# Half-array pairs for the gated layers' up slabs and Strassen products, with the products between an up slab's two passes

## The chip, the cores and the metric

The kernel runs on one core of a Trainium2 chip. The metric is the device time of one execution in microseconds, here the median of three runs. The engines are TensorE (PE; the profile shows its weight loads apart as PEld), VectorE (DVE), ScalarE (ACT), GpSimd (POOL) and SyncE (SP, which issues the DMAs). All of them work through their own instruction streams in order and meet only at semaphores.

## The reference, cut to what matters

A decoder trunk of two layers on 512 tokens of width 1024, in fp32. Each layer is a gated feed-forward half, a mixer, and another gated half; after each the residual sum is normalised:

```
def swiglu(x, w1, w3, w2):
    return (jax.nn.silu(x @ w1) * (x @ w3)) @ w2

h = swiglu(x, ffn_w1[l, 0], ffn_w3[l, 0], ffn_w2[l, 0])      # w1, w3: 1024 x 2816, w2: 2816 x 1024
x = layer_norm(DEEPNORM_ALPHA * x + FFN_RES_WEIGHT * h, ln_g[l, 0], ln_b[l, 0])
```

The mixer of layer 0 is windowed and block-sparse attention, that of layer 1 a gated linear recurrence. The change touches only the four gated (swiglu) layers.

## The kernel before, in words

**Numbers.** Every fp32 operand of the large products is split into a high part of type fp32r (ACT copies it) and a low part, the difference (POOL or DVE subtracts). A product is then three matmuls into one PSUM bank: high by high, high by low, low by high (`three`, L1480 to L1484). All have 128 rows, 128 stationary columns and 512 moving columns in the stretches that matter here. PE loads the stationary operand anew for each.

**A gated layer.** The 2816 hidden features are cut into 11 groups of 256 (`NG`). For each group there is an up slab of w1 (1024 x 256) and one of w3: `up` (L1510) multiplies its two halves j = 0, 1 of 128 features, 8 chunks of the contraction by three matmuls each, 24 matmuls into bank b0 + j, 48 for the slab. w1 slabs use banks 0 and 1, w3 slabs banks 2 and 3. ACT turns banks 0 and 1 into the gate (`gates`, L769), DVE multiplies banks 2 and 3 with it into the hidden tiles (`hiddens`, L1004), into `hid` and `hid_odd` by turns.

The down products of the first eight groups go by Strassen's scheme in Winograd's form. Two groups make one p (p = 0 to 3). The left operand is split into A11, A12, A21, A22 (hidden features by token halves), the right one, two down slabs, into B11 to B22; DVE makes the sums S1 to S4 and T1 to T4 (`left_sum` L1019, `right_sum` L1035), ACT the high parts (L779, L788), DVE the low parts (`left_low` L1025, `right_low` L1041). Seven products P1 to P7 replace eight: each (`product`, L1517) is 12 matmuls, 6 for each of two token tiles t, tile t into bank b0 + t, the banks being 4, 5 and 6, 7 by turns. DVE then adds them to x or keeps them (`add_product` L1057, `keep_product` L1066 and L1069). At p = 3 `combine_kept` follows.

**Order on PE** (L1821 on), with s0 the layer's first slab: slabs 0 to 3, then for each p: slab 4p+4, P1, P2; slab 4p+5, P6, P5; slab 4p+6, P7, P3; slab 4p+7, P4. Then come the last slabs and the ordinary down products. Before each piece PE waits for the operands' counts (`lo_ready` for a slab; `left_lo_ready` and `right_lo_ready` for a product) and for its banks (`gate_done`, `hid_done`, `product_added`).

**Order on the others.** DVE, from the end of slab 4p+3: two hidden tiles, sums S1, S3, S2, low part of A12, sum S4, add P4 of the p before, low parts of S1, B11, S2, S3, S4, A22, the four right sums, then keep P1, add P2, low parts T2, T1; after slab 4p+5: two hidden tiles, low part of the next A11 (at p = 3 of a whole hidden tile instead), keep P6, low T3, add P5, low B22, add P7 and P3, low T4 and the next B21. ACT: high parts in the same order, the gates, and the high copy of one slab (L755) in four places of each p; the copy of slab s waits until the slab two before has released its slot (`w_free`). POOL: the low part of each slab in four quarters (L684, `low`), in order, as soon as ACT has made the high part. SP loads slabs as their buffers come free.

Of the kernel before, what the change touches and what calls it, by code (L numbers as in the profile page):

```python
# [31 lines left out]
P = 128  # L32
# [4 lines left out]
DC = D // P  # L37
GW = 256
NG = DFF // GW
# [10 lines left out]
HALF_CHUNK = 64  # L50
# [11 lines left out]
NP = 4  # L62
# [5 lines left out]
PRODUCTS = ["P1", "P2", "P6", "P5", "P7", "P3", "P4"]  # L68
LEFT = {"P1": "A11", "P2": "A12", "P3": "S4", "P4": "A22", "P5": "S1", "P6": "S2", "P7": "S3"}
# [132 lines left out]
def build_trunk(nc, x_in, w1, w3, w2, ln_g, ln_b, aw_in, sinks, aw_out, hw_in, hnorm, hw_out, lbs_in, out,  # L202
# [7 lines left out]
    for n, ph in enumerate(phases):  # L210
        s0 = bases[n][0]
# [14 lines left out]
    with ExitStack() as ctx:  # L226
# [3 lines left out]
        def sem(name):  # L230
            return ctx.enter_context(nc.semaphore(name))
# [132 lines left out]
        right_lo_ready = sem("right_lo_ready")  # L364
        product_done = sem("product_done")
        product_added = sem("product_added")
        kept_combined = sem("kept_combined")
        y_added = sem("y_added")
        par_loaded = [sem(f"par_loaded{i}") for i in range(2)]
# [50 lines left out]
        def added_count(f, p, name, i):  # L420

            return N_ADDED * (NP * f + p) + ADDED[name] + i

        def left_count(f, p, name):

            return 7 * (NP * f + p) + LEFT_ORDER.index(name) + 1

        def right_count(f, p, name):

            return 7 * (NP * f + p) + RIGHT_ORDER.index(name) + 1  # L430
# [1048 lines left out]
        def _(pe):  # L1479
            def three(out_, w, xs, first, last):  # L1480

                pe.matmul(out_, w[0], xs[0], start=first, stop=False)  # L1482
                pe.matmul(out_, w[0], xs[1], start=False, stop=False)  # L1483
                return pe.matmul(out_, w[1], xs[0], start=False, stop=last)  # L1484
# [29 lines left out]
                    pe.wait_ge(freed, 2 * G - 1 + j)  # L1514
                    features(bank[b0 + j], slot_of[s], j, slice(0, T)).then_inc(done, 1)

            def product(n, f, p, name, b0):  # L1517

                a_hi_, a_lo_ = left_parts(LEFT[name])
                b_hi_, b_lo_ = right_parts(n, RIGHT[name])  # L1520
                pe.wait_ge(left_lo_ready, left_count(f, p, LEFT[name]))
                pe.wait_ge(right_lo_ready, right_count(f, p, RIGHT[name]))
                at = PRODUCTS.index(name)
                q, last_user = (p, PRODUCTS[at - 2]) if at >= 2 else (p - 1, ("P4", "P3")[at])
                for t in range(2):
                    tok = slice(t * P, (t + 1) * P)
                    if q >= 0:
                        n_targets = (2, 1)[last_user not in ("P5", "P7")]
                        pe.wait_ge(product_added, added_count(f, q, last_user, n_targets * (t + 1)))
                    for c in range(2):  # L1530
                        mm = three(bank[b0 + t][:], (a_hi_[:, c, tok], a_lo_[:, c, tok]),
                                   (b_hi_[:, c, :], b_lo_[:, c, :]), c == 0, c == 1)
                    mm.then_inc(product_done, 1)

            def keep_clock(times):

# [276 lines left out]
            for n, (kind, _, _, _) in enumerate(phases):  # L1813
                s0, K0, H0 = bases[n]
                if kind == "ffn":
# [4 lines left out]
                    up(s0 + 3, G0 + 1, up3_done, hid_done, 2)  # L1820
                    for p in range(NP):  # L1821
                        G = G0 + 2 * p + 2
                        up(s0 + 4 * p + 4, G, up1_done, gate_done, 0)
                        product(n, fi, p, "P1", 4)
                        product(n, fi, p, "P2", 6)
                        up(s0 + 4 * p + 5, G, up3_done, hid_done, 2)
                        product(n, fi, p, "P6", 4)
                        product(n, fi, p, "P5", 6)
                        up(s0 + 4 * p + 6, G + 1, up1_done, gate_done, 0)
                        product(n, fi, p, "P7", 4)  # L1830
                        product(n, fi, p, "P3", 6)
                        up(s0 + 4 * p + 7, G + 1, up3_done, hid_done, 2)
                        product(n, fi, p, "P4", 4)

                    G = G0 + NG - 1
                    up(s0 + UPS - 1, G, up1_done, gate_done, 0)
# [77 lines left out]
```

## Time and profile before

| | us |
|---|---|
| median of 3 runs (lowest to highest) | 1984.76 (1984.67 to 1986.42) |
| the profiled execution, whole | 1986.88 |
| its span in the trace | 1984.8 |
| PE busy | 1951.8 (98%) |
| weight loads busy (beside matmuls) | 1657.4 (84%) |
| DVE busy | 1090.4 (55%) |
| ACT busy | 631.9 (32%) |
| POOL busy | 909.4 (46%) |

Busy times are unions over an engine's instructions, so overlapping matmuls are not counted twice. A matmul's duration in the profile runs from its start until its result is in PSUM; since matmuls are pipelined, what one costs is read from the distance between two starts. The granted clock is given as a share of full speed: 1.00 is 2.4 GHz, 0.50 is 1.2 GHz.

### The profile page before, as it was taken

The numbers are of one execution on the slowest core, as the hardware profiler recorded it, in microseconds if no ns is written. First come the engines' busy times: TensorE is split into PE (matmuls) and PEld (weight loads), VectorE is DVE, ScalarE is ACT, GpSimd is POOL, SyncE is SP. The second block draws the span as 40 slices with busy tenths as digits, with TensorE's granted clock in tenths as the row PEclk, the third lists the DMA queues.
The fourth block names the chain that finished last, engine by engine and source line by source line (L and its number), as shares of the span: only waits on it lengthen the run. The fifth ranks groups of instructions, "written<-read, shape, count | busy, mean of one in ns | idle before, by whom it ended". The sixth has DMA issues, their size and how long they took to land.

```text
span 1984.8 us, 26090 instructions
## 1 busy us (share of the span) xinstructions
PE 1951.8 (98%) x10825; PEld 1657.4 (84%) x10825; DVE 1090.4 (55%) x1492; ACT 631.9 (32%) x789; POOL 909.4 (46%) x600
## 2 busy tenths in 40 slices
PE   8999999999999999999999999999999999999997
PEld 8888888978878888888988888898988888888886
DVE  2756472544364766563575647265544774656545
ACT  3333232253422333322333323232232223323321
POOL 4454464632314455355445446453433344365534
PEclk9999999999999999999999999999999999999999
DMA  6232323221104232232423132332221204333221
GB/s 236 97 107 71 128 85 106 90 69 60 64 22 149 85 106 94 98 106 85 149 85 106 64 128 85 106 100 71 68 83 65 64 28 143 107 98 114 92 79 43
DMA packets 135589, 185.52 MB, mean 93 GB/s; under 512 B 3232, under 2 KB 119088, under 8 KB 135472
## 3 DMA queue, kind: packets, MB, share of 16 engines
q1 hardware_dynamic: 135312, 183.59, 27.9%
q8 instruction: 86, 1.41, 0.3%
q10 hardware_dynamic: 160, 0.26, 0.1%
q14 instruction: 31, 0.25, 0.0%
HBM read 181.48 MB, written 2.10 MB: 92 GB/s over the span
## 4 chain that ended last, share of the span: by engine, by line
PE 94%; DVE 4%; DMA 1%; ACT 0%; issue 0%; SPq 0%; POOL 0%; DVEq 0%; ACTq 0%
PE psum L1482 30%; PE psum L1483 29%; PE psum L1484 29%; PE psum L1771 2%; PE psum L1743 1%; PE psum L1710 1%; PE psum L1506 1%; PE psum L1725 1%; DVE x L1097 1%; DMA raw<-in_ffn_w 1%; DVE arena L1199 0%; DVE arena L1200 0%; PE psum L1799 0%; DVE x L1276 0%; PE psum L1809 0%
## 5 line engine op out<-in xcount | busy, mean ns | idle before, releaser
L684 POOL TENSOR_TENSOR w_lo<-raw,w_hi 128x512 fp32r<-128x512 f32 x524 | 849.1, 1652 | 921.6 <-ACT w_hi L755 897.1
L1482 PE MATMUL psum<-xt_hi,w_hi 128*128 128x512 f32 (+1 forms) x1824 | 676.3, 371 | 2.6 <-DVE xt_lo L996 1.2
L1484 PE MATMUL psum<-xt_hi,w_lo 128*128 128x512 f32 (+1 forms) x1824 | 671.5, 368 | 0.0
L1483 PE MATMUL psum<-xt_lo,w_hi 128*128 128x512 f32 (+1 forms) x1824 | 671.5, 368 | 0.0
L1482 PEld LDWEIGHTS psum<-xt_hi,w_hi 128*128 128x128 f32 x1824 | 344.4, 189 | 65.1 <-issue 4.0
L1484 PEld LDWEIGHTS psum<-xt_hi,w_lo 128*128 128x128 f32 x1824 | 344.3, 189 | 57.4
L1483 PEld LDWEIGHTS psum<-xt_lo,w_hi 128*128 128x128 f32 x1824 | 344.5, 189 | 55.8
L755 ACT ACTIVATE w_hi<-raw 128x2048 fp32r<-128x2048 f32 x132 | 251.8, 1911 | 325.8 <-PE psum L1484 323.9
L1057 DVE SCALAR_TENSOR_TENSOR x<-psum,x 128x512 f32<-128x512 f32 x224 | 145.6, 684 | 131.5 <-PE psum L1484 128.3
L769 ACT ACTIVATE gate<-psum 128x512 f32<-128x512 f32 x88 | 52.5, 597 | 308.8 <-PE psum L1484 308.8
L1097 DVE SCALAR_TENSOR_TENSOR x<-psum,x 128x512 f32<-128x512 f32 x128 | 85.9, 687 | 108.5 <-PE psum L1484 108.2
L1482 PE MATMUL psum<-w_hi,h_hi 128*128 128x512 f32 x352 | 140.1, 398 | 2.9 <-DVE x L1097 2.8
L1482 PE MATMUL psum<-w_hi,xt_hi 128*128 128x256 f32 (+2 forms) x448 | 140.7, 314 | 0.0
L1483 PE MATMUL psum<-w_lo,h_hi 128*128 128x512 f32 x352 | 138.4, 393 | 0.0
L1484 PE MATMUL psum<-w_hi,xt_lo 128*128 128x256 f32 (+2 forms) x448 | 137.4, 307 | 0.0
L1483 PE MATMUL psum<-w_lo,xt_hi 128*128 128x256 f32 (+2 forms) x448 | 137.3, 306 | 0.0
L1484 PE MATMUL psum<-w_hi,h_lo 128*128 128x512 f32 x352 | 137.1, 390 | 0.0
L1483 PE MATMUL psum<-w_lo,a_hi 128*128 128x512 f32 x320 | 126.1, 394 | 0.0
L1482 PE MATMUL psum<-w_hi,a_hi 128*128 128x512 f32 x320 | 125.4, 392 | 0.0
L1484 PE MATMUL psum<-w_hi,a_lo 128*128 128x512 f32 x320 | 124.2, 388 | 0.0
L1041 DVE TENSOR_TENSOR w_lo<-raw_odd,w_hi 128x1024 fp32r<-128x1024 f32 x48 | 59.1, 1231 | 110.5 <-ACT w_hi L788 110.5
L1004 DVE TENSOR_TENSOR hid<-psum,gate 128x512 f32<-128x512 f32 x48 | 33.2, 691 | 151.2 <-PE psum L1484 151.2
(168 smaller groups left out, 2199.1 us busy)
## 6 DMA issues: line engine op xcount, KB each, us to landing
raw<-in_ffn_w SPq DMA_DIRECT2D x115, 1024.0 KB, 5.4
raw_odd<-in_ffn_w SPq DMA_DIRECT2D x16, 1024.0 KB, 5.1
raw<-in_hgrn_w_in SPq DMA_DIRECT2D x16, 1024.0 KB, 5.4
raw<-in_attn_w_in SPq DMA_DIRECT2D x9, 1024.0 KB, 5.3
raw<-in_attn_w_out SPq DMA_DIRECT2D x4, 1024.0 KB, 4.9
raw<-in_hgrn_w_out SPq DMA_DIRECT2D x4, 1024.0 KB, 4.9
lng<-in_ln_g SPq DMA_DIRECT2D x6, 512.0 KB, 4.2
lnb<-in_ln_b SPq DMA_DIRECT2D x6, 512.0 KB, 5.9
```

The source lines that it names most:

```text
L684: op = pool.tensor_tensor(w_lo[:, slot_of[s], cols], raw[:, slot_of[s], cols], w_hi[:, slot_of[s], cols].bitcast(F32), ALU.subtract)
L755: act.activation(w_hi[:, slot_of[s], :], raw[:, slot_of[s], :], ACT.Copy).then_inc(hi_ready, 1)
L769: act.activation(gate[:, j, :], bank[j][:], ACT.Silu).then_inc(gate_done, 1)
L1004: dve.tensor_tensor(dst[:, j, :], bank[2 + j][:], gate[:, j, :], ALU.mult).then_inc(hid_done, 1)
L1041: dve.tensor_tensor(lo, right_source(n, name), hi.bitcast(F32), ALU.subtract).then_inc(right_lo_ready, 1)
L1057: dve.scalar_tensor_tensor(out=x_piece(row, t, half), in0=bank[b0 + t][:], scalar=weight / ALPHA, in1=x_piece(row, t, half), op0=ALU.mult, ...
L1097: dve.scalar_tensor_tensor(out=part, in0=banks[k % len(banks)][:], scalar=weight / ALPHA, in1=part, op0=ALU.mult, op1=ALU.add).then_inc(y_ ...
L1482: pe.matmul(out_, w[0], xs[0], start=first, stop=False)
L1483: pe.matmul(out_, w[0], xs[1], start=False, stop=False)
L1484: return pe.matmul(out_, w[1], xs[0], start=False, stop=last)
L1506: mm = pe.transpose(bank[4 + 2 * (t % 2) + b][:, c * P:(c + 1) * P], x[:, t, (4 * b + c) * P:(4 * b + c + 1) * P], ident[:])
L1771: mm = pe.matmul(out_, ks[:, g % 2, h, keys], rhs, start=True, stop=True)
```

## The change

`three` is kept for everything else. For slabs 4p+4 to 4p+7 and for all seven products each full matmul becomes two matmuls over 64 of the 128 rows. A new helper, `crossed`, emits them in pairs: one of the pair uses rows 0 to 63 and one output bank, the other rows 64 to 127 and the other output bank. In the first pass output o = 0 takes the lower rows and o = 1 the upper, in the second pass the other way round, so that after both passes each bank holds the sum over all 128 rows. The second pass waits for a semaphore that the last matmul of the first raises. Both banks' `done` counts are raised together at the end of the second pass. Between the two passes of a slab stand the first passes of its products, and after the slab's second pass the products' second passes. Operands and free banks are waited for before the first pass, for both outputs at once.

```diff
--- before.py
+++ after.py
@@ -364,6 +364,9 @@
         right_lo_ready = sem("right_lo_ready")
         product_done = sem("product_done")
         product_added = sem("product_added")
+        up1_half_done = sem("up1_half_done")
+        up3_half_done = sem("up3_half_done")
+        product_half_done = sem("product_half_done")
         kept_combined = sem("kept_combined")
         y_added = sem("y_added")
         par_loaded = [sem(f"par_loaded{i}") for i in range(2)]
@@ -1514,23 +1517,57 @@
                     pe.wait_ge(freed, 2 * G - 1 + j)
                     features(bank[b0 + j], slot_of[s], j, slice(0, T)).then_inc(done, 1)
 
-            def product(n, f, p, name, b0):
+            def crossed(outs, operands, steps, second):
+
+
+                for c in range(steps):
+                    for a, b in ((0, 0), (0, 1), (1, 0)):
+                        for o in range(2):
+                            half = 1 - o if second else o
+                            rows = slice(half * HALF_CHUNK, (half + 1) * HALF_CHUNK)
+                            w, xs = operands(o, c)
+                            mm = pe.matmul(outs[o][:], w[a][rows], xs[b][rows],
+                                           start=not second and c == 0 and a + b == 0,
+                                           stop=second and c == steps - 1 and a == 1)
+                return mm
+
+            def up_half(second, s, f, G, done, half_done, freed, b0):
+
+                if second:
+                    pe.wait_ge(half_done, 2 * NP * f + G - NG * f - 1)
+                else:
+                    pe.wait_ge(lo_ready, s + 1)
+                    pe.wait_ge(freed, 2 * G)
+                slot = slot_of[s]
+
+                def operands(j, c):
+                    cols = slice(c * GW + j * P, c * GW + (j + 1) * P)
+                    return (w_hi[:, slot, cols], w_lo[:, slot, cols]), (xt_hi[:, c, :], xt_lo[:, c, :])
+
+                mm = crossed((bank[b0], bank[b0 + 1]), operands, DC, second)
+                mm.then_inc(*((done, 2) if second else (half_done, 1)))
+
+            def product_half(second, n, f, p, name, b0):
 
                 a_hi_, a_lo_ = left_parts(LEFT[name])
                 b_hi_, b_lo_ = right_parts(n, RIGHT[name])
-                pe.wait_ge(left_lo_ready, left_count(f, p, LEFT[name]))
-                pe.wait_ge(right_lo_ready, right_count(f, p, RIGHT[name]))
                 at = PRODUCTS.index(name)
-                q, last_user = (p, PRODUCTS[at - 2]) if at >= 2 else (p - 1, ("P4", "P3")[at])
-                for t in range(2):
-                    tok = slice(t * P, (t + 1) * P)
+                if second:
+                    pe.wait_ge(product_half_done, 7 * (NP * f + p) + at + 1)
+                else:
+                    pe.wait_ge(left_lo_ready, left_count(f, p, LEFT[name]))
+                    pe.wait_ge(right_lo_ready, right_count(f, p, RIGHT[name]))
+                    q, last_user = (p, PRODUCTS[at - 2]) if at >= 2 else (p - 1, ("P4", "P3")[at])
                     if q >= 0:
                         n_targets = (2, 1)[last_user not in ("P5", "P7")]
-                        pe.wait_ge(product_added, added_count(f, q, last_user, n_targets * (t + 1)))
-                    for c in range(2):
-                        mm = three(bank[b0 + t][:], (a_hi_[:, c, tok], a_lo_[:, c, tok]),
-                                   (b_hi_[:, c, :], b_lo_[:, c, :]), c == 0, c == 1)
-                    mm.then_inc(product_done, 1)
+                        pe.wait_ge(product_added, added_count(f, q, last_user, 2 * n_targets))
+
+                def operands(t, c):
+                    tok = slice(t * P, (t + 1) * P)
+                    return (a_hi_[:, c, tok], a_lo_[:, c, tok]), (b_hi_[:, c, :], b_lo_[:, c, :])
+
+                mm = crossed((bank[b0], bank[b0 + 1]), operands, 2, second)
+                mm.then_inc(*((product_done, 2) if second else (product_half_done, 1)))
 
             def keep_clock(times):
 
@@ -1820,17 +1857,21 @@
                     up(s0 + 3, G0 + 1, up3_done, hid_done, 2)
                     for p in range(NP):
                         G = G0 + 2 * p + 2
-                        up(s0 + 4 * p + 4, G, up1_done, gate_done, 0)
-                        product(n, fi, p, "P1", 4)
-                        product(n, fi, p, "P2", 6)
-                        up(s0 + 4 * p + 5, G, up3_done, hid_done, 2)
-                        product(n, fi, p, "P6", 4)
-                        product(n, fi, p, "P5", 6)
-                        up(s0 + 4 * p + 6, G + 1, up1_done, gate_done, 0)
-                        product(n, fi, p, "P7", 4)
-                        product(n, fi, p, "P3", 6)
-                        up(s0 + 4 * p + 7, G + 1, up3_done, hid_done, 2)
-                        product(n, fi, p, "P4", 4)
+                        for second in (False, True):
+                            up_half(second, s0 + 4 * p + 4, fi, G, up1_done, up1_half_done, gate_done, 0)
+                            product_half(second, n, fi, p, "P1", 4)
+                            product_half(second, n, fi, p, "P2", 6)
+                        for second in (False, True):
+                            up_half(second, s0 + 4 * p + 5, fi, G, up3_done, up3_half_done, hid_done, 2)
+                            product_half(second, n, fi, p, "P6", 4)
+                            product_half(second, n, fi, p, "P5", 6)
+                        for second in (False, True):
+                            up_half(second, s0 + 4 * p + 6, fi, G + 1, up1_done, up1_half_done, gate_done, 0)
+                            product_half(second, n, fi, p, "P7", 4)
+                            product_half(second, n, fi, p, "P3", 6)
+                        for second in (False, True):
+                            up_half(second, s0 + 4 * p + 7, fi, G + 1, up3_done, up3_half_done, hid_done, 2)
+                            product_half(second, n, fi, p, "P4", 4)
 
                     G = G0 + NG - 1
                     up(s0 + UPS - 1, G, up1_done, gate_done, 0)
```

## Rows read from the trace of the kernel before

**Rows 1.** Part 1 of the page: busy us, share, instructions.

```profile
PE 1951.8 (98%) x10825; PEld 1657.4 (84%) x10825; DVE 1090.4 (55%) x1492; ACT 631.9 (32%) x789; POOL 909.4 (46%) x600
```

**Rows 2.** Part 4 of the page: chain that ended last, by engine.

```profile
PE 94%; DVE 4%; DMA 1%; ACT 0%; issue 0%; SPq 0%; POOL 0%; DVEq 0%; ACTq 0%
```

**Rows 3.** Windows: window, length, busy by engine, clock, DMA share, GB/s.

```profile
59.61:321.48 261.87, 261.87 (x1153) 216.26 (x1152) 158.05 (x187) 85.65 (x90) 130.55 (x68) 1.00 0.29 96
```

**Rows 4.** Timeline of PE (start, length): slab 4 and P1, first matmuls.

```profile
59.62 0.39 PE L1482 MATMUL psum<-xt_hi,w_hi 128*128 128x512 f32 x1
...
70.50 0.39 PE L1482 MATMUL psum<-w_hi,h_hi 128*128 128x512 f32 x1
```

**Rows 5.** Timeline of PE: 256-column matmuls, first and last of 43.

```profile
380.78 0.28 PE L1484 MATMUL psum<-xt_hi,w_lo 128*128 128x256 f32 x1
...
385.81 0.28 PE L1484 MATMUL psum<-xt_hi,w_lo 128*128 128x256 f32 x1
```

**Rows 6.** Timeline of PE: P4 first, next slab first, 12 matmuls apart.

```profile
182.36 0.39 PE L1482 MATMUL psum<-w_hi,a_hi 128*128 128x512 f32 x1
...
185.11 0.39 PE L1482 MATMUL psum<-xt_hi,w_hi 128*128 128x512 f32 x1
```

**Rows 7.** Groups of PE by form: scores (count, busy us, mean ns).

```profile
L1710 PE MATMUL psum<-arena 64*128 64x512 f32 x16 | 4.5, 641 | 0.0
...
L1710 PE MATMUL psum<-arena 64*128 64x384 f32 x16 | 3.7, 535 | 0.0
```

**Rows 8.** Timeline of PE and PEld: scores on alternating halves, merged.

```profile
540.27 1.13 PE L1710 MATMUL psum<-arena 64*128 64x512 f32 x4
...
549.06 0.93 PE L1710 MATMUL psum<-arena 64*128 64x128 f32 x8
549.16 0.42 PEld L1710 LDWEIGHTS psum<-arena 64*128 64x128 f32 x6
```

**Rows 9.** Timeline of DVE and POOL, p = 0 of the first layer.

```profile
59.88 0.69 DVE L1004 TENSOR_TENSOR hid_odd<-psum,gate 128x512 f32<-128x512 f32 x1 [4.75 <-PE psum L1484]
...
62.43 1.79 DVE L1025 TENSOR_TENSOR h_lo<-hid_odd,h_hi 128x512 fp32r<-128x512 f32 x1
...
67.54 2.31 DVE L1041 TENSOR_TENSOR w_lo<-raw,w_hi 128x1024 fp32r<-128x1024 f32 x1
...
61.87 6.89 POOL L684 TENSOR_TENSOR w_lo<-raw,w_hi 128x512 fp32r<-128x512 f32 x4 [14.08 <-ACT w_hi L755]
```

**Rows 10.** Timeline of DVE, beginning of p = 2.

```profile
182.63 0.69 DVE L1004 TENSOR_TENSOR hid_odd<-psum,gate 128x512 f32<-128x512 f32 x1 [0.97 <-PE psum L1484]
...
188.18 1.22 DVE L1041 TENSOR_TENSOR w_lo<-raw,w_hi 128x1024 fp32r<-128x1024 f32 x1
...
195.34 2.10 DVE L1035 TENSOR_TENSOR raw_odd<-raw_odd,raw 128x1024 f32<-128x1024 f32 x1
```

**Rows 11.** Timeline of POOL: slab 4p+5 of p=2, two quarters.

```profile
188.26 8.11 POOL L684 TENSOR_TENSOR w_lo<-raw,w_hi 128x512 fp32r<-128x512 f32 x1 [13.56 <-ACT w_hi L755]
...
199.82 1.30 POOL L684 TENSOR_TENSOR w_lo<-raw,w_hi 128x512 fp32r<-128x512 f32 x1
```

**Rows 12.** Timeline of PE: first matmul of slab 4p+5, p = 2.

```profile
201.48 0.39 PE L1482 MATMUL psum<-xt_hi,w_hi 128*128 128x512 f32 x1
```

**Rows 13.** Timeline of DVE, p=2: hidden tile of slab 4p+5, B22.

```profile
212.63 0.69 DVE L1004 TENSOR_TENSOR hid<-psum,gate 128x512 f32<-128x512 f32 x1 [4.37 <-PE psum L1484]
...
221.11 1.21 DVE L1041 TENSOR_TENSOR w_lo<-raw_odd,w_hi 128x1024 fp32r<-128x1024 f32 x1
```

**Rows 14.** Timeline of DVE, p = 3: the same two.

```profile
275.38 0.69 DVE L1004 TENSOR_TENSOR hid<-psum,gate 128x512 f32<-128x512 f32 x1 [4.75 <-PE psum L1484]
...
285.57 1.21 DVE L1041 TENSOR_TENSOR w_lo<-raw_odd,w_hi 128x1024 fp32r<-128x1024 f32 x1
```

**Rows 15.** Timeline: PE after its longest idle; window there (columns: group 3).

```profile
1370.55 0.64 PE L1771 MATMUL psum<-arena 128*64 128x32 f32 x8 [2.66 <-DVE arena L1201]
...
1370.00:1376.80 6.80, 6.25 (x42) 5.26 (x43) 3.80 (x8) 0.00 (x0) 2.90 (x3) 0.50 0.36 117
```

## The prediction

> **What bounds the kernel now.** I read the busy line first [rows 1]: TensorE (PE) is busy 98% of the span, and PE makes up 94% of the chain that ended last [rows 2]. In the four gated layers the stretch that the change touches is full: from slab 4 of the first layer to its first down product PE is busy 261.87 of 261.87 us at clock 1.00 [rows 3], and the other three are alike. So two things can move the time: what a matmul costs, and whether PE still finds its operands when it asks for them.
>
> What one costs: 48 matmuls of 512 columns start between 59.62 and 70.50 us, 226.7 ns apart [rows 4]. 42 intervals of 256-column ones take 380.78 to 385.81 us, 119.8 each [rows 5]. So 256 more columns cost 106.7 ns. 512 columns stream in 213.3, which is the level of 2.4 GHz at one column per cycle, and 13.3 ns are left between two weights. A Strassen product of 12 matmuls runs from 182.36 to 185.11: 229 ns each [rows 6].
>
> **What a pair of half matmuls costs.** Changed are 64 up slabs (4 per p, 4 p, 4 layers) of 48 matmuls, 3072, and 112 products of 12, 1344. Each becomes two 64-row matmuls on different halves and banks. Columns per half are as many as before, so a pair never takes less than 213.3, and at best 13.3 (15.7 in a product) are saved: 3072 x 13.3 + 1344 x 15.7 = 62 us. The nearest rows are the attention scores, 64-row matmuls of plain fp32 on alternating halves and two banks, where each is two instructions. From 384 to 512 columns their mean grows by 106 ns [rows 7], so they stream half as fast (427 for 512). Four that stream 853 ns a half lie within 1.13 us, eight that stream 640 within 0.93 [rows 8]: the halves do run together. Both carry the same first load and last drain, the one has 1 change of weights, the other 3: 1.13 - 0.853 = 0.277, 0.93 - 0.640 = 0.290, so 13 ns for two changes, 6.5 each. Bounds: 213.3 (change fully hidden) and 226.7 (these are fp32, and the 13.3 may belong to the fp32r operands). I take 213.3 + 6.5 = 219.8, by these rows. Gain: 3072 x 6.9 + 1344 x 9.2 = 34 us, 8.4 a layer.
>
> The trace's 226.7 also stands against a rule. The Trainium skill ("TensorE: Matmul & The Clock Gate", Back-to-back issue gap) has 512/2.4 + 2.5 = 215.8 ns between matmuls at the high clock; no row here shows that for 512 columns, and were a pair to reach it, the gain would be 51 us.
>
> **What the new order asks of the other engines.** One p is four slots: slab 4p+4 with P1, P2; 4p+5 with P6, P5; 4p+6 with P7, P3; 4p+7 with P4. Before, a product started after its whole slab, 10.88 us into the slot. Its first half now starts after half the slab, 24 x 0.2198 = 5.28 us in, and needs all its operands then. A half product takes 1.32, a slot 15.83, the last 13.19 (before 16.37 and 13.63). The operands come from queues of ACT, DVE and POOL that nothing shortens. I lay them against PE.
>
> *p = 0, P1.* The chain begins at slab 3, which is untouched: DVE starts the second hidden tile at 59.88, and right_low of B11 starts at 67.54 and takes 2.31, to 69.85 [rows 9]. Before, P1 asked at 70.50, 0.65 later. Now it asks at 59.62 + 5.28 = 64.9, and waits 5.0 us. Behind it in PE's queue stand P2, the slab's second pass and everything else, and no buffer or other work fills the hole. DVE is late because it shares its port: POOL works on slab 5 from 61.87, and DVE's operations of 0.68 take 1.79 [rows 9].
>
> *Boundary, p = 1 to 3.* Count from the end U of the second pass of the last slab (4p+7 of the p before). P4's second half ends at 1.32, the next slab's first pass at 6.60: there P1 asks. Slot 2 asks for slab 4p+5 at 1.32 + 15.83 = 17.15. Before, the hidden tile j=0 was done long before, and j=1 began 0.27 after the slab (182.36 to 182.63 [rows 6, 10]). Now both are released together, so j=1 begins at 0.27 + 0.60 = 0.87. From it DVE runs without a pause: B11's low part starts 5.55 after j=1 and takes 1.22 (188.18), so it is ready at 7.64 and P1 waits 1.1. Then come four left and four right sums, the last ending at 197.44, 14.8 after j=1 [rows 10]. Under these POOL's first quarter of slab 4p+5, released by ACT's high copy, took 8.11 us where the last took 1.30, and the slab was ready at 201.12, 18.5 after j=1 [rows 11]. PE used it at 201.48 [rows 12]: a slack of 0.36. Now 0.87 + 18.5 = 19.4 against 17.15: 2.25 us late. The wait of P1 lies within that, so it counts once. ACT is some 0.6 earlier, since P4 ends earlier after the slab, so POOL may come just as DVE reads PSUM and get the port at once. Then B11 becomes late as at p = 0 (two operations longer by 1.1 each: P1 waits 3.3) and the slab is in time. Ends 1.1 and 3.3; I take 2.25.
>
> *Slot 3, P3.* Before, B22's low part starts 8.48 after the hidden tile and takes 1.21, so it ends 9.69 after [rows 13]. That tile's chain is started by ACT's high copy, which the slab's end releases, so it isn't shifted by the 0.60. In the new slot 2 the slab ends at 13.19, B22 is ready at 13.19 + 0.27 + 9.69 = 23.15, and P3 asks at 15.83 + 5.28 + 1.32 = 22.43: 0.8 late with the wait's own latency. At p = 3 the two low parts of a whole hidden tile stand ahead (10.19 + 1.21 = 11.4 after, [rows 14]): 1.7 more, 2.5.
>
> Nothing else is late: P6 asks for T2 2 us or more after it is ready, P4 for T4 1.4 after; B21 comes 7.3 after T4, before the hidden tiles. The gates, now two at a time, are a slot ahead. Slabs 4p+6 to 4p+8 had 7 us or more to spare. A slab's weights come free 2.3 us later, which only 4p+5 could feel, and its copy waits for other work anyway. SP's loads hang on low parts that move with PE. The second pass's wait on the first (half_done) is covered by the products between them, 1.3 us or more; without that it would cost the drain, 0.39 - 0.21 = 0.18 us each.
>
> Stalls a layer: 5.0 + 3 x 2.25 + 3 x 0.8 + 2.5 = 16.7; four layers 67 us, twice the gain.
>
> *Clock.* After the one idle stretch of PE of 2.66 us (it ended at 1370.55) the granted clock is 0.50, 1.2 GHz, from 1370.0 to 1376.8 [rows 15]. The 5.0 us hole of p = 0 is longer. At half clock 3.4 to 6.8 us of work cost 1.7 to 3.4 more; bounds 0 and 3.4, I take 2.5: 10 us for four. Changes between full and half arrays, eight of them: about 0.1 each by the load no longer hidden, 1 us.
>
> **Sum.** -34 + 67 + 10 + 1 = +44 us. The profiled execution took 1986.88 (span 1984.8), 2 above the median 1984.76 of the three timed. 1986.88 + 44 = 2031; against the median 2029. I forecast 2028.
>
> **Rivals.**
> *Change of weights wholly hidden (213.3).* Gain 62. The halves' loads may overlap the other half's stream entirely. But PE then asks earlier: P1 5.1 late, the boundary 16.64 against 19.4 (2.75), slot 3 1.05, at p = 3 2.75: 19.3 a layer, 77. -62 + 77 + 11 = +26: 2011.
> *No cheaper pair (226.7).* Gain 3, from the products only; stalls 4.75 + 3 x 1.7 + 3 x 0.5 + 2.2 = 13.6 a layer, 54. +62: 2047. For it: 13.3 was only seen with fp32r, 6.5 only with fp32. It would also come about if half loads ran one after the other, about 0.11 each, twice in a pair. Against: six score loads of 0.19 lie in 0.42 us [rows 8], 0.115 a pair. The Trainium skill (same page, LDWEIGHTS) says that a load costs by its columns, not its rows, so that the change doubles the loading; by those rows the two loads of a pair overlap.
> *The port falls the other way (not slower).* If at p = 0 POOL is starved as it is at 188.26, DVE's operations stay at 0.6 to 1.2 and P1 waits 1.8; if at the boundary POOL gets in during DVE's PSUM reads and gives way again, slab 4p+5 is in time and 1.1 is left. Stalls 1.8 + 3.3 + 2.4 + 2.5 = 10 a layer, holes too short for the clock: at 219.8 that is 40 - 34 + 1 = +7. With 213.3, 46 - 62 + 1 = -15: 1970. It decides from a pair price of about 217.7 down. Against: at p = 0 the order on ACT, DVE and POOL is untouched.
> *The halves take turns.* Each half matmul at 226.7: 4416 x 226.7 = +1000 us, 2985. Only possible if fp32r behaves unlike the scores, which write each PSUM column at half the rate.
>
> **How the numbers follow.** Forecast 56%, its own range 2012 to 2048 (stalls 1.1 to 3.3 at twelve boundaries, clock 0 to 14). Fully hidden 14%, no cheaper 10%, port 15%, turns 5%. Range 1998 to 2060, which holds the first three with their spread (longer holes at boundaries may drop the clock too). 0.2% is about what a measurement can tell. Faster: 11 of the port's 15. Same: 3 of them. Slower: the rest, 86%.
>
> **What would show it.** In the changed profile: (1) a pair's starts 219.8 apart, its two matmuls some 7 ns apart; (2) an idle of 5.0 us of PE before P1 of p = 0, ended by DVE w_lo L1041, in each layer; (3) idle before slot 2 of p = 1 to 3, ended by POOL's low part, and a shorter one before P1; (4) 0.8 and 2.5 us before P3, ended by DVE; (5) a clock of 0.50 after the hole (2). PE without idle in the stretch, whatever the pair costs, would prove me wrong; so would pairs above 227.

## The result and the profile after

The changed kernel takes 2067.85 us (three runs, 2065.39 to 2069.22) against 1984.76 before: ratio 1.0415, 95% interval 1.0395 to 1.0436. It is slower by 83 us; the forecast was 2028, slower by 43, with a range up to 2060. The direction was right, and most of the places where PE waits; the size was not.

The page's busy line, after (compare [rows 1]), and its chain by engine ([rows 2]):

```profile
PE 1980.5 (96%) x15241; PEld 1786.6 (86%) x15241; DVE 1121.4 (54%) x1492; ACT 619.2 (30%) x789; POOL 838.8 (41%) x600
...
PE 89%; DVE 7%; issue 3%; ACT 1%; DMA 0%; SPq 0%; POOL 0%; DVEq 0%; ACTq 0%
```

PE has 4416 matmuls more and is busy 28.7 us more, in a span that is 81 us longer: most of the loss is idle. Windows of the first gated layer (length, then busy time of PE, PEld, DVE, ACT, POOL, clock, DMA share, GB/s), the first from its slab 4 to its first down product ([rows 3] before):

```profile
59.47:343.01 283.54, 270.63 (x2257) 247.36 (x2257) 165.87 (x187) 82.40 (x90) 113.15 (x68) 0.98 0.28 89
68.59:75.41 6.82, 5.71 (x27) 4.86 (x29) 6.78 (x8) 0.00 (x0) 0.00 (x0) 0.50 0.52 154
269.97:273.38 3.41, 3.41 (x20) 3.08 (x18) 3.41 (x3) 0.00 (x0) 3.37 (x3) 0.50 0.00 0
307.52:310.93 3.41, 3.41 (x19) 3.18 (x16) 3.38 (x6) 0.00 (x0) 0.00 (x0) 0.50 0.51 174
```

The stretch grew from 261.87 to 283.54 us: 13 us without a matmul, and three windows at half clock. Over four layers the same stretches are longer by 21.7, 19.8, 21.7 and 19.1, 82 us together, which is the whole difference.

What a pair costs, PE's timeline (each row is the two halves of a pair, their starts 10 ns apart):

```profile
84.09 0.40 PE L1529 MATMUL psum<-xt_hi,w_hi 64*128 64x512 f32 x2
84.31 0.40 PE L1529 MATMUL psum<-xt_lo,w_hi 64*128 64x512 f32 x2
...
84.99 0.40 PE L1529 MATMUL psum<-xt_lo,w_hi 64*128 64x512 f32 x2
```

The halves do run together, but a pair starts every 226.7 ns, the distance of the full matmuls before ([rows 4]): a half-slab of 24 pairs takes 5.44 us, a product 2.75. Nothing is gained.

The holes, that is, the stretches in which PE stands idle (PE, then DVE): P1 at p = 0, P1 at p = 1, and P3 at p = 3.

```profile
64.84 0.39 PE L1529 MATMUL psum<-xt_hi,w_lo 64*128 64x512 f32 x2
69.70 0.79 PE L1529 MATMUL psum<-w_hi,h_hi 64*128 64x512 f32 x2 [4.48 <-DVE w_lo L1044]
...
135.59 0.43 PE L1529 MATMUL psum<-xt_hi,w_lo 64*128 64x512 f32 x2
137.87 0.50 PE L1529 MATMUL psum<-w_hi,h_hi 64*128 64x512 f32 x2 [1.84 <-issue]
...
306.99 0.50 PE L1529 MATMUL psum<-w_hi,a_hi 64*128 64x512 f32 x2 [1.87 <-DVE w_lo L1044]
```

```profile
67.28 2.28 DVE L1044 TENSOR_TENSOR w_lo<-raw,w_hi 128x1024 fp32r<-128x1024 f32 x1
...
134.86 0.68 DVE L1028 TENSOR_TENSOR a_lo<-left_sum,a_hi 128x512 fp32r<-128x512 f32 x1
135.46 2.31 DVE L1044 TENSOR_TENSOR w_lo<-raw,w_hi 128x1024 fp32r<-128x1024 f32 x1
```

At p = 0 DVE ends B11's low part at 69.56 and P1 starts at 69.70 (forecast: 5.0 late; a start-to-start distance of 4.86, less the 0.23 of a pair, is 4.6). At the boundary between two p the low part ends at 137.77, P1 starts at 137.87, though the profile names no releaser ("issue"). POOL came in just before it:

```profile
134.90 7.42 POOL L687 TENSOR_TENSOR w_lo<-raw,w_hi 128x512 fp32r<-128x512 f32 x4 [11.64 <-ACT w_hi L758]
```

Against [rows 11], where the first quarter alone took 8.11, all four take 7.42. This time POOL is not held up, so slab 4p+5 is ready over 6 us early, and B11's low part is longer by 1.1. That is the case which the prediction gave as its upper end of 3.3, but one operation is longer, not two, and the wait is 2.0. POOL began while DVE was ending an addition that reads PSUM (at 134.94); that this is what let it in is argued, no run tests it.

### The profile page after: what moved, and what is told of

The parts are those of the page before. It is cut to its first block, busy times and chain, and to the rows that moved or that the text cites. A ratio compares the mean times of both kernels' runs of the same rounds, so it can differ in the third digit from the quotient of the medians.

```text
span 2065.8 us, 34922 instructions
## 1 busy us (share of the span) xinstructions
PE 1980.5 (96%) x15241; PEld 1786.6 (86%) x15241; DVE 1121.4 (54%) x1492; ACT 619.2 (30%) x789; POOL 838.8 (41%) x600
## 4 chain that ended last, share of the span: by engine, by line
PE 89%; DVE 7%; issue 3%; ACT 1%; DMA 0%; SPq 0%; POOL 0%; DVEq 0%; ACTq 0%
PE psum L1529 47%; PE psum L1485 12%; PE psum L1486 12%; PE psum L1487 12%; PE psum L1808 2%; PE psum L1780 1%; PE psum L1747 1%; DVE w_lo L1044 1%; PE psum L1509 1%; PE psum L1762 1%; DVE x L1100 1%; DMA raw<-in_ffn_w 0%; DVE arena L1202 0%; DVE arena L1203 0%; DVE x L1060 0%
## 5 line engine op out<-in xcount | busy, mean ns | idle before, releaser
L1529 PE MATMUL psum<-xt_hi,w_hi 64*128 64x512 f32 x2048 | 432.8, 388 | 0.0
L1529 PE MATMUL psum<-xt_lo,w_hi 64*128 64x512 f32 x2048 | 431.3, 387 | 0.0
L1529 PE MATMUL psum<-xt_hi,w_lo 64*128 64x512 f32 x2048 | 431.2, 387 | 0.0
L1485 PE MATMUL psum<-xt_hi,w_hi 128*128 128x512 f32 (+1 forms) x800 | 278.0, 348 | 2.9 <-DVE w_lo L1353 1.2
L1487 PE MATMUL psum<-xt_hi,w_lo 128*128 128x512 f32 (+1 forms) x800 | 272.8, 341 | 0.0
L1486 PE MATMUL psum<-xt_lo,w_hi 128*128 128x512 f32 (+1 forms) x800 | 272.7, 341 | 0.0
L1529 PEld LDWEIGHTS psum<-xt_hi,w_hi 64*128 64x128 f32 x2048 | 225.3, 185 | 14.6 <-issue 1.4
L1529 PEld LDWEIGHTS psum<-xt_lo,w_hi 64*128 64x128 f32 x2048 | 225.0, 185 | 13.0
L1529 PEld LDWEIGHTS psum<-xt_hi,w_lo 64*128 64x128 f32 x2048 | 224.2, 184 | 13.0
L1485 PEld LDWEIGHTS psum<-xt_hi,w_hi 128*128 128x128 f32 x800 | 151.8, 190 | 26.6 <-issue 5.4
```

The lines of the kernel that those rows point to most:

```text
L1529: mm = pe.matmul(outs[o][:], w[a][rows], xs[b][rows], start=not second and c == 0 and a + b == 0, stop=second and c == steps - 1 and a == 1)
```

## The experiments

**Order or halves?** The first pair of kernels separates the change's two parts. e1 keeps the new order and has full matmuls:

```diff
-                for c in range(steps):
+                for c in range(steps // 2 * second, steps // 2 * (second + 1)):
                     for a, b in ((0, 0), (0, 1), (1, 0)):
                         for o in range(2):
-                            half = 1 - o if second else o
-                            rows = slice(half * HALF_CHUNK, (half + 1) * HALF_CHUNK)
...
-                            mm = pe.matmul(outs[o][:], w[a][rows], xs[b][rows],
+                            mm = pe.matmul(outs[o][:], w[a], xs[b],
```

> The changed kernel's order kept exactly (slab in two passes, the first passes of its products between them, operands and banks waited for before the first pass, both banks' counts raised at the end), but with full 128-row matmuls: a pass takes half of the contraction's chunks for both outputs. Theory (a pair of halves costs just what a full matmul costs, and all of the loss is the order): no difference from the changed kernel, 2068 us (2060 to 2076), with the same idle before P1 at p = 0 (about 4.7 us) and at the boundaries (about 2.0 us). Rival (the halves themselves cost something, in loads, drains or clock): clearly below 2060, by what they cost.

2065.43 us (ratio to before 1.0409, 1.0392 to 1.0426), and the hole before P1 stands at 4.73 us idle. PE's timeline at the hole:

```profile
68.94 0.70 PE L1526 MATMUL psum<-w_hi,h_hi 128*128 128x512 f32 x2 [4.73 <-DVE w_lo L1044]
```

The halves can be taken away and the loss stays: it is the order's. e2 keeps the halves and has the old order:

```diff
                         for second in (False, True):
                             up_half(second, s0 + 4 * p + 4, fi, G, up1_done, up1_half_done, gate_done, 0)
+                        for second in (False, True):
                             product_half(second, n, fi, p, "P1", 4)
                             product_half(second, n, fi, p, "P2", 6)
```

(and so for the other three slabs).

> Half-array pairs as in the changed kernel, but each slab's second pass follows its first at once, and the products come after the whole slab as before the change. Theory (order is the cause): before 1984.8, minus 3 for the products at 226.7, plus 5 waits of a second pass on the first per p that nothing covers now (4 slabs and P4), 80 in all at about 0.2 us: 16, plus some 4 at the boundaries where both hidden tiles are still released together and at mode changes: 2001 us (1994 to 2010), without the 4.7 us hole. Rival (half pairs are the cause): stays near 2068.

2016.28 (ratio 1.0157, 1.0142 to 1.0173), 31 us above before, where I had expected 16. The holes are gone and no window in the layers is at half clock. PE's timeline where a slab's second pass begins:

```profile
64.42 0.39 PE L1529 MATMUL psum<-xt_hi,w_lo 64*128 64x512 f32 x2
64.87 0.50 PE L1529 MATMUL psum<-xt_hi,w_hi 64*128 64x512 f32 x2
65.20 0.40 PE L1529 MATMUL psum<-xt_lo,w_hi 64*128 64x512 f32 x2
```

The rest is this uncovered wait: the two steps take 0.45 and 0.33 us instead of 0.23 each, and a slab's 48 pairs take 11.24 us for 10.88. So a second pass that nothing covers costs 0.36 us and not 0.2; 80 of them are 29 us. The drain (the end of a matmul's recorded duration, in which the next one could already stream), by which I had sized it, is only half of what it costs: the weight loads, which elsewhere start with the matmul before, start here only after the wait.

**What the holes do to the clock.** e4 puts half-array matmuls of no use in front of P1's and P3's waits, where PE was idle:

```diff
                 else:
+                    fill = {("P1", 0): 19, ("P3", 3): 7}.get((name, p), 7 if name == "P1" else 0)
...
+                    for i in range(fill):
+                        for o in range(2):
+                            rows = slice(o * HALF_CHUNK, (o + 1) * HALF_CHUNK)
+                            pe.matmul(bank[6 + o][:], xt_hi[rows, i % 8, 0:P], xt_hi[rows, i % 8, :],
+                                      start=True, stop=True)
                     pe.wait_ge(left_lo_ready, left_count(f, p, LEFT[name]))
```

> The changed kernel with half-array matmuls of no use put before P1 (19 pairs at p = 0, 7 else) and before P3 at p = 3 (7), where PE stood idle; into banks 6 and 7, which are free. They end before the operands come. Theory (the holes drop the clock, and the time at 1.2 GHz after them costs 20 us: half of 39 us of work in the ten windows at 0.50 within the changed stretches): 2048 us (2042 to 2055), no window at 0.50 in those stretches. Rival (the clock's drops come from elsewhere or cost little): within 4 us of 2068.

2051.14 (ratio 1.0332, 1.0316 to 1.0347): 16.7 less than the changed kernel, by doing more. The first layer's window has clock 1.00 throughout:

```profile
59.10:340.00 280.90, 278.00 (x2362) 248.72 (x2362) 166.20 (x188) 84.77 (x93) 113.30 (x68) 1.00 0.28 91
```

So the half clock after the holes cost some 17 to 20 us, where the prediction had 10: 17 is the whole gain of e4, and its waits are some 3 us longer than the changed kernel's. Each layer's stretch is still 16.4 longer than before: 65 us for the waits themselves.

**Why DVE is late at p = 0.** e7 moves one ACT copy, and with it POOL's work on slab 5:

```diff
-                        if p == 0:
-                            high(s0 + 5)
                         left_high(fi, p, "A12")
...
                         for name in ("S2", "S3", "S4", "A22"):
                             left_high(fi, p, name)
+                        if p == 0:
+                            high(s0 + 5)
```

> The changed kernel with one move: at p = 0 ACT copies slab 5 (and so releases POOL's part of it) after the high parts of S2 to A22 and not before A12's. Theory (the hole at p = 0 is so long because POOL's subtraction shares DVE's port while DVE makes B11's operands): DVE's operations up to B11 take 0.6 and 1.2 us, B11 is ready about 3 us earlier, the hole before P1 shrinks from 4.7 to about 1.6 us and stops dropping the clock (some 2.4 us more a layer): 2068 - 4 x 5.4 = 2046 us (2042 to 2058). Rival (DVE is slowed by something else, such as ACT's copies or PE's reads): the hole stays 4 us or more, 2064 to 2070.

2045.72 (ratio 1.0307, 1.0291 to 1.0322). DVE's timeline, from the hidden tile on:

```profile
58.69 0.69 DVE L1007 TENSOR_TENSOR hid_odd<-psum,gate 128x512 f32<-128x512 f32 x1 [4.75 <-PE psum L1487]
...
61.22 0.69 DVE L1028 TENSOR_TENSOR h_lo<-hid_odd,h_hi 128x512 fp32r<-128x512 f32 x1
61.83 0.68 DVE L1022 TENSOR_TENSOR hid_odd<-hid_odd,hid 128x512 f32<-128x512 f32 x1
62.43 0.69 DVE L1028 TENSOR_TENSOR a_lo<-left_sum,a_hi 128x512 fp32r<-128x512 f32 x1
63.03 1.22 DVE L1044 TENSOR_TENSOR w_lo<-raw,w_hi 128x1024 fp32r<-128x1024 f32 x1
```

B11 is ready 5.56 us after the hidden tile begins, where it took 9.9 to 10.0 with POOL at work beside it ([rows 9]). That it is POOL and not ACT shows in the same rows: ACT copies high parts in both kernels while DVE works, and DVE's operations are long only while POOL subtracts (61.63 to 68.47 in the changed kernel; here POOL begins at 65.68). So the time of an operand is set by another engine's work beside it. The 4.3 us gained are more than the 3 I had expected, and P1 is only 0.3 late. In exchange slab 5 itself is now late, 0.4 us of idle in each layer.

**Are the holes only the queues' order?** e5 leaves PE as changed and reorders ACT and DVE:

```diff
-                        left_low(fi, p, "A12")
-                        left_sum(fi, p, "S4")
                         if p:
                             add_product(fi, p - 1, "P4", 4, [(1, 0)], weight)
+                            right_low(n, fi, p, "B11")
+                        left_low(fi, p, "A12")
+                        left_sum(fi, p, "S4")
                         left_low(fi, p, "S1")
-                        right_low(n, fi, p, "B11")
```

(ACT alike; at p = 0 B11's low part stands before the loop; the low part of the next A11, at p = 3 of a whole hidden tile, moves behind B22's.)

> The changed kernel, PE's order untouched; only ACT and DVE are reordered: B11's high and low part before A12's (at p = 0 before the hidden tiles), the addition of P4 ahead of them, and the low part of the next A11 (at p = 3 of a whole hidden tile) behind B22's. Theory (the holes are these queues' order): the holes before P1 (4.7 us at p = 0, 2.0 else) and before P3 go, and with them the windows at half clock; as a pair costs what a full matmul costs, the time comes back to that of before and no further: 1984 to 1992 us, if slab 4p+5 stays in time; if POOL now starves as it did before the change, up to 2 us at each of 12 boundaries come back: up to 2016. Rival (the holes move to the next operand, P2's or T2): above 2030.

1996.78 (ratio 1.0067, 1.005 to 1.0083): 71 of the 83 us are back, and no window of the layers is at half clock. That is above the 1984 to 1992 expected. What is left is 12 waits of 0.5 us or a little more at p = 1 to 3, before P5's first half in slot 2, one of 1.0 and small ones. The profile names no releaser for them:

```profile
145.22 0.43 PE L1530 MATMUL psum<-w_hi,a_lo 64*128 64x512 f32 x2
146.00 0.51 PE L1530 MATMUL psum<-w_hi,a_hi 64*128 64x512 f32 x2 [0.34 <-issue]
```

It ends above the kernel before: when a pair costs what a full matmul costs, nothing can bring it below.

**Where the 13.3 ns lie.** They are the excess of a matmul's 226.7 ns over the 213.3 in which its columns stream. Two probes stand behind the last down product of the kernel before; each kind has 18 to 36 matmuls, pairs or quadruples.

```diff
                     last_downs(n, s0 + UPS + 2, K0 + 1, H0 + 2)
+                        for i in range(36):
+                            pe.matmul(bank[2], st(LO, i), mv(LO, i), start=True, stop=True)
+                            pe.matmul(bank[3], st(HI, i), mv(HI, i), start=True, stop=True)
...
```

> The kernel before, with extra matmuls of 512 columns behind its last down product, each kind 18 to 36 times from operands that lie in SBUF (its output is untouched). Distance between starts read for each. Theory (the 13.3 ns beside the 213.3 of streaming belong to every fp32r matmul in every row group that it uses): full array with the same stationary operand each time 227, alternating banks 227, pair of halves 227 a pair, one half alone 227, four 32-row groups 227 a quadruple, 64 stationary columns 227; plain fp32 full arrays and pairs both about 427 + 6 an instruction. Rival A (the 13.3 are the change of the stationary operand): less with the same operand or with 64 columns. Rival B (they are the bank's): less where banks alternate. The Trainium skill (TensorE: Matmul & The Clock Gate, Back-to-back issue gap) gives 215.8 for a moving operand of 512 columns; if the type makes the 13.3, the bf16 cases show it, full and paired.

PE's timeline, merged by line (banks by turns; one half alone; four 32-row groups; 64 stationary columns; contiguous bf16):

```profile
1987.71 8.32 PE L1852 MATMUL psum<-xt_hi,w_hi 128*128 128x512 f32 x36
...
2004.28 8.32 PE L1857 MATMUL psum<-xt_hi,w_hi 64*128 64x512 f32 x36
2012.53 5.76 PE L1861 MATMUL psum<-xt_hi,w_hi 32*128 32x512 f32 x96
2018.21 8.49 PE L1863 MATMUL psum<-xt_hi,w_hi 128*64 128x512 f32 x36
2026.78 7.72 PE L1865 MATMUL psum<-xt_hi,w_hi 128*128 128x512 bf16 x35
```

Less the last one's 0.39 and divided by the steps between, these are 226.6 with alternating banks, 226.6 for one half alone, and 215.9 for bf16 (its row has 35 of 36). Where the kind changes, the first step can be longer; from the second start on it is 227 for a quadruple of row groups and 230 with 64 columns. The same stationary operand each time gave 226.7, pairs of bf16 halves 216, plain fp32 429.1 an instruction full and 429.2 in halves. So it is neither the change of weights nor the bank nor the number of rows. The 215.8 of the Trainium skill (TensorE: Matmul & The Clock Gate, Back-to-back issue gap) holds here for contiguous bf16 and not for fp32r.

Is it the type? e8 and e9 below use bf16 at a stride of 4 bytes, where a matmul took 225. The second probe tells type and stride apart:

> A second probe behind the kernel before, full arrays, 24 to 36 matmuls of each kind. In e9 the cross terms, bf16 read at a stride of 4 bytes, took 225 ns each, and the first probe's contiguous bf16 216. Theory (the 10 ns or more beyond streaming go with how far the moving operand's 512 elements are spread, 2048 bytes a row, whatever the type): bf16 with a strided moving operand and contiguous stationary 225, with a contiguous moving and a strided stationary 216; fp32r with one column repeated 512 times (stride 0) near 216; fp32r at a stride of 8 bytes 227 or more. Rival (it is the type, and in e9 the stationary stride costs the 9 ns): the other way round for the two bf16 cases, and 227 for fp32r at every stride. 384 and 256 columns of fp32r: 160 + 13 = 173 and 120 as in the kernel if the excess is per matmul, 170 and 113 if it is per column.

```profile
1979.66 8.30 PE L1851 MATMUL psum<-xt_hi,w_hi 128*128 128x512 bf16 x36
1987.80 7.93 PE L1854 MATMUL psum<-xt_hi,w_hi 128*128 128x512 bf16 x36
1995.38 16.59 PE L1857 MATMUL psum<-xt_hi,w_hi 128*128 128x512 f32 x36
...
2008.63 2.89 PE L1857 MATMUL psum<-xt_hi,w_hi 128*128 128x512 f32 x6
...
2011.79 8.03 PE L1859 MATMUL psum<-xt_hi,w_hi 128*128 128x512 f32 x36
2019.66 6.43 PE L1861 MATMUL psum<-xt_hi,w_hi 128*128 128x384 f32 x36
2025.92 4.47 PE L1863 MATMUL psum<-xt_hi,w_hi 128*128 128x256 f32 x36
2030.23 4.26 PE L1865 MATMUL psum<-xt_hi,w_hi 128*128 128x256 bf16 x36
```

In this order: bf16 with a strided moving operand 226, bf16 with a strided stationary operand 216, fp32r at a stride of 8 bytes 452 (the six from its middle; its first step takes 0.60), fp32r with one column repeated 218, fp32r with 384 columns 174, with 256 120, bf16 strided with 256 columns 113. So at 512 columns the excess of fp32r and of bf16 goes with how the moving operand lies in memory, 4 bytes from element to element, and not with which of the two types it is; at 8 bytes a matmul takes twice as long. In fp32r the excess is the same for 512, 384 and 256 columns (13 to 14 ns), but in strided bf16 it is 12 to 13 at 512 and 7 at 256: what sets it with fewer columns stays open. Plain fp32 lies 4 bytes apart as well and has an excess of only 2.5 over its 426.7; there each column takes two cycles. Both halves of the array read moving operands that are spread in the same way. That this is why a pair keeps the 13.3 fits the pairs of contiguous bf16, which come to 216; strided pairs of bf16 were not run.

**A faster version.** If the type were the cause, the cross terms could be read as bf16 from the words that are there. These kernels ran before the second probe. e6 does it in each triple, on the kernel before. A bf16 keeps the upper 16 bits of the word:

```diff
+                def top(part):
+                    return part.bitcast(mybir.dt.bfloat16)[..., 1::2]
+
                 pe.matmul(out_, w[0], xs[0], start=first, stop=False)
-                pe.matmul(out_, w[0], xs[1], start=False, stop=False)
-                return pe.matmul(out_, w[1], xs[0], start=False, stop=last)
+                pe.matmul(out_, top(w[0]), top(xs[1]), start=False, stop=False)
+                return pe.matmul(out_, top(w[1]), top(xs[0]), start=False, stop=last)
```

> The kernel before (full arrays, old order) with the two cross terms of each fp32r triple read as bf16, the upper 16 bits of the same words, no new copies. The products high by high stay fp32r. Theory (13.3 ns belong to the fp32r type, 2.6 to bf16, as in the probe): 5060 matmuls or so of 512 columns are cross terms, 10.8 ns less each: 55 us less, and PE's slack towards slab 4p+5 was 0.36 us only, so at 12 boundaries most of the gain of their stretch (84 matmuls x 2/3 x 10.8 = 0.6 us) is lost again: 1932 us (1922 to 1950). Rival (a stride of 4 bytes between bf16 elements costs PE's reads, or a change of type between matmuls costs a gap): no faster than 1985, or slower.

2022.53 (ratio 1.0189, 1.0174 to 1.0204), slower: a triple takes 700 ns where three full fp32r matmuls take 680. Its rows show the gap at the change of type, since the fp32r matmul begins 26 ns after the last bf16 one and the next begins only 430 later:

```profile
80.11 0.39 PE L1487 MATMUL psum<-xt_hi,w_lo 128*128 128x512 bf16 x1
80.14 0.59 PE L1485 MATMUL psum<-xt_hi,w_hi 128*128 128x512 f32 x1
80.57 0.40 PE L1486 MATMUL psum<-xt_lo,w_hi 128*128 128x512 bf16 x1
```

e8 groups them in all of these products, the mixers' too, so that the type changes once for two banks. e9 moves one of ACT's copies besides (the second part of the edit):

```diff
+            def grouped(out_, operands, first, last, cross_first):
+                calls = [(w[0], xs[0]) for w, xs in operands]
+                cross = [x for w, xs in operands for x in ((top(w[0]), top(xs[1])), (top(w[1]), top(xs[0])))]
+                calls = cross + calls if cross_first else calls + cross
...
                         left_high(fi, p, "A12")
+                        if p:
+                            high(s0 + 4 * p + 5)
                         left_high(fi, p, "S1")
                         right_high(n, fi, p, "B11")
-                        if p:
-                            high(s0 + 4 * p + 5)
```

> The kernel before (full arrays, old order). In every bank the fp32r products high by high of all chunks stand together, and the cross terms together, read as bf16 (upper 16 bits of the same words); the second bank of a pair begins with its cross terms, so that the type changes to and fro once for two banks. Theory (a bf16 matmul of 512 columns takes 215.9, an fp32r one 226.7, and what made e6 slower is one change of type per triple, some 40 ns for each round trip: 700 ns measured against 658): an up slab saves 32 x 10.8 - 42 = 0.30 us, 80 of them 24; a product 0.045; first slabs and mixers about 10 together; in all 38, of which the boundaries of p, where PE had 0.36 us to spare towards slab 4p+5, take back 12 x 1.2 = 14: 1961 us (1950 to 1975). Rival (the loss in e6 is the bf16 read at a stride of 4 bytes, each matmul): not below 1985.

> As e8, and ACT's high copy of slab 4p+5 (p = 1 to 3) stands directly behind A12's, before S1's and B11's. Theory (POOL then comes while DVE reads PSUM, gets the port, and the slab is in time; B11 is some 3 us later, which the old order of PE has to spare): the 14 us of the boundaries are not lost: 1947 us (1938 to 1960), PE without idle before slot 2. Rival (B11 or the right sums become late instead): as slow as e8 or slower.

1975.33 (ratio 0.9948, 0.9933 to 0.9963) and 1973.35 (0.9937, 0.992 to 0.9954). Both beat the kernel before, by 10 and 12 us, but the forecasts of 1961 and 1947 were far too good. Part of the reason is the price of a bf16 matmul:

```profile
95.17 0.39 PE L1495 MATMUL psum<-xt_lo,w_hi 128*128 128x512 bf16 x1
95.39 0.39 PE L1495 MATMUL psum<-xt_hi,w_lo 128*128 128x512 bf16 x1
95.62 0.39 PE L1495 MATMUL psum<-xt_lo,w_hi 128*128 128x512 bf16 x1
```

It is 225 ns, not 216: the stride keeps most of the excess. e9 had nothing left to win: the 14 us at the boundaries that it was to bring back were not lost in e8, where PE is busy 260.00 of 260.00 us from 60 to 320. Matmuls of 256 columns went from 120 to 113 and those of 128 columns from about 109 to 57. For these the fp32r load (188 ns against 98 in bf16) may have set the pace; no run tests it. The cross terms carry fewer bits than before in e6, e8 and e9.

## Why the prediction was wrong, step by step

*The price of a pair: the step that failed.* The prediction took 213.3 + 6.5 = 219.8 from the scores and a gain of 34 us. Measured are 226.7 a pair and 229 in a product, no gain at all. The scores are plain fp32, which streams a column in two cycles, and the probe gives such matmuls an excess of 2.5 ns in full arrays as in halves (429 against 426.7): their small excess was a property of the operand and not of the half array. The 6.5 was also half of a difference of 13 ns between two rows that are read to 10 ns. The price came out at the upper bound, and "no cheaper pair" was the rival that came true, for the reason it gave first, that the 13.3 belong to the fp32r operands (at 512 columns by their layout, as the second probe shows, not their type). Its second reason, half loads one after the other, is not seen. Its price, 2047, was 21 us short: the products were not 3 us cheaper, the clock cost 20 and not 10, and the waits 62 and not 54.

*The waits.* Forecast 67 us at 219.8 and 54 at 226.7; the stretches without their clock loss are 62 us longer (82 less 20), and 65 in e4. Item by item, a layer: P1 at p = 0, 4.8 forecast at 226.7, 4.6 found; boundary 1.7, found 2.0; P3 0.5 and 2.2, found 0.5 and 2.0. These items come to 56 us; of the other 6 about 3 lie in the first step after each wait, which takes 0.31 where 0.23 is usual, and the rest was not followed. The chain from the hidden tile through DVE's queue to B11 could be laid out beforehand to within 0.3 us. At the boundary the place was wrong: not slab 4p+5 but P1 was late, since POOL was not held up. That 2.0 lies so near the 2.25 forecast there is luck: the two are waits for different operands.

*The clock.* Forecast 10 us, half of the 20 found (half of 39.6 us of work in ten windows at 0.50). I had counted only the hole of p = 0, and for it the 2.5 a layer were right: the four windows there cost 9.6 us. The other 10 come from the waits of 1.8 to 2.2 us at P1 and P3, which were followed by a half-clock window in 6 of 16 places (such as 269.97 and 307.52) and in the others not (such as after 137.87 and 203.40). Waits of 2.25 and 2.5 us stood in the prediction, with room in its range but no term in its sum for the clock; and its port rival called holes of 1.8 us too short for the clock, which they are not.

Together: pair price +34, clock +10, waits -5: 44 becomes 83. The range had room for each, but not for both on top of each other. Of its signs, (2) and (4) came, a little smaller than told, (5) came more often than told, and (1) and the idle before slot 2 in (3) did not come.

*Right:* the covers named for T2, T4, B21, the gates and SP's loads held; no other wait came up.

## What to carry to other kernels

Before an operation is split to hide an overhead, find out what the overhead belongs to: a price read from another operand type is a bound and no estimate. And when work on the bound engine is moved forward, lay out the queue of each engine that makes its operands, with the time at which the first operand is asked for; here the order of a few operations on DVE and ACT was worth 71 us, the halves nothing.

## What the runs showed of the hardware

- A matmul of 512 columns costs 226.7 ns in fp32r, whose moving operand's elements lie 4 bytes apart, and 226 in bf16 at that stride; it costs 216 in bf16 when they lie 2 apart, 452 in fp32r at 8, and 218 in fp32r when one column is repeated. The stationary operand's stride makes no difference in bf16 (216).
- Two halves of the array write two banks, and four row groups four banks, at the full rate at once: 227 for a pair, 227 for a quadruple.
- Going from bf16 to fp32r and back costs some 23 ns: 700 for a triple of e6, against 226.7 + 2 x 225 = 677. (The 40 of e8's expectation took 216 for the bf16 ones.)
- A wait of PE on its own last matmul costs 0.36 us between two runs of pairs (e2), twice the drain in its recorded duration.
- An idle of 1.8 to 2.2 us in a stretch of dense matmuls was followed by 3.4 us at half clock in 6 of 16 places, one of 4.5 us in 4 of 4. Filling them with matmuls of no use made the kernel 17 us faster.
- A DVE subtraction of 128x512 takes 0.68 us alone and 1.79 beside POOL's, where POOL is not held up; where POOL is held up, DVE keeps its 0.68 and a quarter of POOL's takes 8.11 for 1.30 ([rows 11]).
